# A two-block transformer kernel on one Trainium2 core: the first projections opened feature chunk by feature chunk

## What is computed

```python
mod = jax.nn.silu(c) @ w_ada + b_ada                       # c: 1 x 1024, w_ada: 1024 x 3072
shift, scale, gate = jnp.split(mod[:, None, :], 3, axis=-1)
h = rms_norm(x, norm_g) * (1 + scale) + shift              # 256 x 1024
z = h @ w_in                                               # w_in: 1024 x 2976
c_q, c_kv, k_rope, g_mla, q_b, k_b, v_b, g_moba = jnp.split(z, list(IN_OFFSETS), axis=-1)
o_mla = mla_attention(c_q, c_kv, k_rope, ...)              # needs the 416 latent columns c_q, c_kv, k_rope
o_moba = moba_attention(q_b, k_b, v_b, ...)                # 8 heads of 64: q, k and v have 512 columns each
y = jnp.concatenate([silu(g_mla) * o_mla, silu(g_moba) * o_moba], axis=-1) @ w_out
return x + gate * y
```

## Time and profile before

| | |
|---|---|
| runs | 1599.12, 1601.88 and 2229.82 us; median 1601.88 us |
| profiled execution | 1596.89 us, its span 1594.7 us |
| TensorE busy | 1552.5 us, 97% of the span |
| VectorE, ScalarE busy | 1069.9 and 869.8 us |
| bytes read | 290.57 MB, 183 GB/s over the span |

### The profile page before, as it was taken

How to read it: one execution, slowest core, us unless ns; L and a number is a source line. 1 busy time by engine, 2 the same in 40 slices (tenths; PEclk the granted TensorE clock), 3 DMA queues, 4 the chain that set the end, 5 groups by cost and what they waited for, 6 DMA issues and landing times.

```text
span 1594.7 us, 21371 instructions
## 1 busy us (share of the span) xinstructions
PE 1552.5 (97%) x7540; PEld 1290.8 (81%) x7540; DVE 1069.9 (67%) x1789; ACT 869.8 (55%) x1534; POOL 117.0 (7%) x142
## 2 busy tenths in 40 slices
PE   4989999999999999999999999999999999999998
PEld 4777887788888888888888888888888888888886
DVE  7987877666555766787756557565666578766553
ACT  3676667455445656565644446444566666554442
POOL 0310021011000000021000001000000002100000
PEclk9999999999999999999999999999999999999999
DMA  9964673379854634546565557975463444665651
GB/s 340 322 233 158 196 239 128 104 180 221 222 185 158 198 96 133 174 141 213 197 200 170 198 184 197 199 205 192 158 199 118 139 160 147 211 207 172 205 184 71
DMA packets 149026, 293.03 MB, mean 184 GB/s; under 512 B 10096, under 2 KB 23184, under 8 KB 148920
## 3 DMA queue, kind: packets, MB, share of 16 engines
q1 hardware_dynamic: 143424, 276.60, 51.5%
q0 software_dynamic: 4352, 12.15, 6.2%
q10 hardware_dynamic: 1144, 2.92, 0.5%
HBM read 290.57 MB, written 1.06 MB: 183 GB/s over the span
## 4 chain that ended last, share of the span: by engine, by line
PE 88%; DVE 5%; ACT 3%; issue 2%; DMA 1%; POOL 0%; DVEq 0%; SPq 0%; ACTq 0%
PE pb L475 83%; PE pb L479 5%; DMA raw<-in_w_ada 1%; DVE wl L1529 1%; ACT wh L906 1%; ACT pb L906 1%; DVE mkv L1526 1%; POOL st L2461 0%; DMA raw<-in_w_in 0%; DVE qt L1526 0%; ACT xt_h L906 0%; DVE mk L1529 0%; ACT mkv L906 0%; DVE B L1529 0%; DVE pb L1532 0%
## 5 line engine op out<-in xcount | busy, mean ns | idle before, releaser
L906 ACT ACTIVATE wh<-raw 128x1024 fp32r<-128x1024 f32 (+1 forms) x484 | 506.5, 1053 | 424.6 <-PE pb L475 394.2
L1529 DVE TENSOR_TENSOR wl<-raw,wh 128x1024 fp32r<-128x1024 f32 (+1 forms) x484 | 581.4, 1218 | 197.6 <-ACT wh L906 193.6
L475 PE MATMUL pb<-wh,xt_h 128*128 128x512 f32 (+2 forms) x1472 | 578.1, 393 | 4.0 <-ACT xt_h L906 2.5
L475 PE MATMUL pb<-wh,xt_l 128*128 128x512 f32 (+2 forms) x1472 | 572.4, 389 | 1.4 <-DVE xt_l L1529 1.0
L475 PE MATMUL pb<-wl,xt_h 128*128 128x512 f32 (+2 forms) x1472 | 569.6, 387 | 0.0
L475 PEld LDWEIGHTS pb<-wh,xt_l 128*128 128x128 f32 x1472 | 277.1, 188 | 64.1 <-DVE xt_l L1526 5.9
L475 PEld LDWEIGHTS pb<-wh,xt_h 128*128 128x128 f32 x1472 | 277.2, 188 | 59.5 <-issue 4.0
L475 PEld LDWEIGHTS pb<-wl,xt_h 128*128 128x128 f32 x1472 | 277.4, 188 | 52.5
L475 PE MATMUL pb<-wh,big_h 128*128 128x512 f32 x352 | 137.7, 391 | 0.0
L475 PE MATMUL pb<-wh,big_l 128*128 128x512 f32 x352 | 137.0, 389 | 0.0
L475 PE MATMUL pb<-wl,big_h 128*128 128x512 f32 x352 | 137.0, 389 | 0.0
(11 more groups left out here) (242 smaller groups left out, 1546.5 us busy)
## 6 DMA issues: line engine op xcount, KB each, us to landing
raw<-in_ffn_w_gu SPq DMA_DIRECT2D x160, 512.0 KB, 4.9
raw<-in_w_in SPq DMA_DIRECT2D x148, 512.0 KB, 4.3
raw<-in_ffn_w_down SPq DMA_DIRECT2D x88, 512.0 KB, 3.9
raw<-in_w_ada SPq DMA_DIRECT2D x48, 512.0 KB, 5.3
raw<-in_w_out SPq DMA_DIRECT2D x32, 512.0 KB, 4.1
raw<-in_w_branch SPq DMA_DIRECT2D x24, 512.0 KB, 4.2
raw<-in_ffn_w_gu SPq DMA_DIRECT2D x32, 256.0 KB, 4.9
raw<-in_w_in SPq DMA_DIRECT2D x8, 416.0 KB, 4.8
```

The source lines that it names most:

```text
L475: return e.matmul(o, a, b, start=start, stop=stop)
L906: return e.activation(o, a, func, **kw)
L1529: return e.tensor_tensor(o, a, b, op)
```

## The change

The opening goes by chunks of 128 features. `w_ada` is loaded as column blocks: for feature chunk kx the 1024x128 block of shift and that of scale, each as one transfer of 128 partitions by 8 pieces of 128 columns (512 bytes a piece in HBM). TensorE makes the shift of the chunk from its block: eight products with 128x128 weights and one moving column (`modulation`). DVE sums the scale block in two partial sums (two TENSOR_SCALAR and six SCALAR_TENSOR_TENSOR of 128x128), and TensorE adds these over the partitions with two products against the column of ones (`modulation_sums`). x is loaded first, by SP, and its normalised transpose is kept in SBUF (`x_turned`, over `mkv`). As each chunk is modulated, z, q and k are added up for it, in six banks. The weights of q and k come as one chunk of 1024 columns, those of z as chunks of two feature rows. The v product follows as before. `keep_busy` is gone. The 24 further rows of `w_ada` all come behind v (`later.over(16)`), and the normalisation and turning of the latents, and `mbias`, come after the turning of the q and k heads. ACT issues all its small loads before its first activation.

```diff
+    x_turned = mkv[:, :, :].rearrange("p a b -> p (a b)").rearrange("p (c n) -> p c n", n=256)
+    part_sums = [[acc[:, 512 * i + 128 * z:512 * i + 128 * z + 128] for z in range(2)] for i in range(2)]
+    ACC_Z, ACC_Q, ACC_K = (0, 1), (2, 3), (6, 7)
...
+        def modulation(kx):
+
+            c = shift_at[kx]
+            b = open_bank(4 + kx % 2, ("modk", kx, 1))
+            w.wait_ge(*at(f"raw{c % NRAW}", c))
+            w.wait_ge(*at("csil"))
+            for cc in range(8):
+                last = mm(b[:, 0:1], chunk_view(raw[c % NRAW], c)[:, cc, :], stat(8, "c_silu")[:, cc:cc + 1], cc == 0, cc == 7)
+            last.then_inc(*up("shm", kx))
+            return b
+
+        def modulation_sums(kx, b):
+
+            w.wait_ge(*at("ones"))
+            w.wait_ge(*at("scs", kx, 7))
+            for z in range(2):
+                last = mm(b[:, 1:2], part_sums[kx % 2][z], ones[:, 0:1], z == 0, z == 1)
+            last.then_inc(*up("modm", kx))
...
-        def keep_busy(n):
-
-            w.wait_ge(*at("x"))
-            for _ in range(n):
-                mm(banks[0][:, 0:256], ident, h[:, 0, 0:256], True, True)
...
-        b = rot("cols")
-        w.wait_ge(*at("rows"))
-        tr(b[:, 0:n_rows], rows[0:n_rows, :]).then_inc(*up("rtr"))
-        turn_row(0, 0)
-        turn_row(0, 1)
-        keep_busy(5)
-        list(rows_of_ada(0, 2))
...
+            def blocks(kx):
+                shift_at[kx] = c_no[0]
+                for j, what in enumerate(("shift", "scale")):
+                    if len(plan) == c_no[0]:
+                        plan.append((wa[:, :, DM * j + 128 * kx:DM * j + 128 * kx + 128], 8, 128, None, None, (what, kx)))
+                    c_no[0] += 1
+
+            def weights(kx):
+                if kx % 2 == 0:
+                    zs[0] = take(wi[:, kx:kx + 2, 0:416], 2, 416, ("mm", ("z", 0), 1) if kx == 6 else None)
+                return take(wi[:, kx:kx + 1, 928:1952], 1, DM, ("mm", ("kb", 0), 1) if kx == 7 else None)
...
+            for kx in range(8):
+                qk = weights(kx)
+                if kx < 7:
+                    blocks(kx + 1)
+                for t in range(2):
...
+                    w.wait_ge(*at("xh", ("x", 0), kx))
+                    for nm, i, c, o, hi, lo in parts:
+                        if kx == 0:
+                            open_bank(i, ("eva", (nm, 0), t))
+                        w.wait_ge(*at("hi", c))
+                        mm(o, xh, hi, kx == 0, False)
+                    for nm, i, c, o, hi, lo in parts:
+                        w.wait_ge(*at("lo", c))
+                        mm(o, xh, lo, False, False)
+                    w.wait_ge(*at("xl", ("x", 0), kx))
+                    for nm, i, c, o, hi, lo in parts:
+                        last = mm(o, xl, hi, False, kx == 7)
+                        if kx == 7:
+                            last.then_inc(*up("mm", (nm, 0), t))
+                        elif t == 1 and nm == "z" and kx % 2 or t == 1 and nm == "kb":
+                            last.then_inc(*up("w", c))
+                    if t == 0 and kx < 7:
+                        modulation_sums(kx + 1, modulation(kx + 1))
...
+            gemm(("vb", l), XT, 0, xkey, win, 1952, 512, "eva")
-                later.over(17)
+                later.add(ada(side_tiles[l]), 10 * len(side_tiles[l]))
+                later.over(16)
...
+            for kx in range(8):
+                w.wait_ge(*at("modk", kx, 1))
+                if kx == 0:
+                    w.wait_ge(*at("xev", 1))
+                if kx == 4:
+                    for t in range(2):
+                        w.wait_ge(*at("xevd", t))
+                affine = {"scale": ac[0][:, kx:kx + 1], "bias": mod[:, 0, kx:kx + 1]}
+                ac_(xt_h[:, kx, :], x_turned[:, kx, :], ACT.Identity, **affine).then_inc(*up("xh", ("x", 0), kx))
+                if kx >= 2:
+                    w.wait_ge(*at("xl", ("x", 0), kx - 2))
+                ac_(xtmp[kx % 2], x_turned[:, kx, :], ACT.Identity, **affine).then_inc(*up("xma", ("x", 0), kx))
+                split(stream.lead(3 if kx % 2 else 4))
...
+            if what[0] == "scale":
+                kx = what[1]
+                if kx >= 2:
+                    w.wait_ge(*at("modm", kx - 2))
+                for cc in range(8):
+                    a, b = part_sums[kx % 2][cc % 2], chunk_view(v, c)[:, cc, :]
+                    weight = stat(8, "c_silu")[:, cc:cc + 1]
+                    if cc < 2:
+                        ts(a, b, weight, None, ALU.mult, None).then_inc(*up("scs", kx, cc))
+                        continue
+                    w.wait_ge(*at("scs", kx, cc - 2))
+                    stt(a, b, weight, a, ALU.mult, ALU.add).then_inc(*up("scs", kx, cc))
+                return
...
+            modulation(0)
+            for kx in range(8):
+                if kx:
+                    modulation(kx)
+                split(stream.lead(1 if kx % 2 else 2))
+                w.wait_ge(*at("xh", ("x", 0), kx))
+                w.wait_ge(*at("xma", ("x", 0), kx))
+                tt(xt_l[:, kx, :], xtmp[kx % 2], xt_h[:, kx, :].bitcast(F), ALU.subtract).then_inc(*up("xl", ("x", 0), kx))
+                if kx < 7:
+                    split(stream.lead(2))
...
+            def opening_steps():
+                for t in range(2):
+                    head_scale("qb", 0, (t,))
+                    head_scale("kb", 512, (t,))
+                    yield
+                steps = z_steps()
+                for _ in range(2):
+                    next(steps)
...
+                side.add(opening_steps(), 4)
+                side.over(4)
             gemm(("vb", l), XT, 8, 512, nothing)
             side.drain()
             if l == 0:
-                later.over(17)
+                later.add(ada(side_tiles[l]), 10 * len(side_tiles[l]))
+                later.over(16)
             turn_heads(4)
             turn_heads(4)
+            if l == 0:
+                c_banks = [rot() for c in range(0, 3, 2)]
+                w.wait_ge(*at("gv"))
+                tt(mbias[:, :, :], gv[:, :, ::-1], same_heads(caus, 8), ALU.add).then_inc(*up("mbias"))
+                lower_latents()
...
+        for t in range(2):
+            e.dma_start(h[:, t, :], d["x"][0, t * 128:t * 128 + 128, :]).then_inc(*landed(f"x{t}"))
```

452 lines of the change are left out of this document (220 added, 232 removed).

## The result

The changed kernel takes 1628.57 us (median of four runs, 1627.66 to 1629.36), the kernel before beside it 1600.5 us. That median takes in one slow run of 2229.82 us; the other three are 1598.92, 1599.12 and 1601.88 us, and the ratio, which leaves the slow one out, is 1.018, 95% interval 1.016 to 1.020: 28 to 29 us slower. In the profiled executions the span grew from 1594.7 to 1627.5 us, by 32.8 us. The prediction said 1618 with 1602 to 1634: the direction and the range held, and the middle was 10 us too low. Of the mechanism the first half held, the longer chunk. The second half, that DVE's backlog behind the opening sets the mark, held for a small part of the delay only, as the experiments show.

A forecast was written before the change was run, and what follows sets the result against it. The opening was taken as bound by bytes, TensorE as the bound behind the mark. Opening to 78.5 us, 65 of DVE work and 3 of waits put the mark at 146.5 against 125.3: 1596.9 + 21 = 1618 us, range 1602 to 1634.

The forecast's parts named there:

- the first half: Opening: engines wait for each other in every feature chunk; 51.0 us from the first modulation to the eighth.
- The second half: Behind the opening: DVE's remaining work, not TensorE's 53 us, sets the mark (`mk` scaled), 21 us later than before.
- Product and piece: Opening chunk: a one-column product costs 0.23 us on TensorE; eight 128x128 scale pieces cost 2.0 us on DVE.
- ACT's pieces: Opening chunk: ACT makes `xt_h` and `dg` in 0.41 us each, with a handover of 0.1.
- Start: Start of the opening: first `ac` at 19.9 us, first weight product between 20 and 23 us.
- Clock: Opening: the first chunk and part of the second run at the lower clock level, 4.2 us more.
- Rival 3: Opening: the clock stays at the lower level throughout; 32 us more, 1650 us; chance 0.08.
- v: Behind z, q and k, complete at 81.2 us: v takes 10.9 us of products and is complete at 92.
- The backlog: From the last `xt_l` at 78.5 us: 65 us of DVE work and 3 us of waits put the mark at 146.5.
- Behind the mark: After `mk` is scaled: both kernels are alike and TensorE is the bound, so nothing gives the delay back.

The follow-up runs named there:

- fillers: Changed kernel with five 256-column products whose result nobody reads put into TensorE's first waits; 1629.85 us.
- thin rows: Changed kernel with the side rows of `w_ada` weighed in one column only, the rows still being read; 1624.54 us.
- one shift product: Changed kernel with only one of the eight one-column products of each chunk's shift sum; 1621.96 us.
- long pieces: Changed kernel with the column blocks of `w_ada` in the opening read in pieces of 4 KB instead of 512 bytes; 1629.3 us.

## Why the prediction came out as it did

**Product and piece.** Both prices held. A one-column product costs two records and 0.23 us: 16 records took 1.84 us in every block, as read from the earlier trace rows. The scale block, bounded between two rows of a different shape, took 25.31 to 27.36, 2.05 us against 2.0.

**ACT's pieces.** `xt_h` and `dg` were put at 0.41 each, from a row that copies. They multiply and add, and took:

```profile
L973 ACT ACTIVATE xt_h<-mkv,mod,ac 128x256 fp32r<-128x256 f32 x8 | 4.8, 601 | 39.0 <-DVE ac L1593 39.0
L973 ACT ACTIVATE dg<-mkv,mod,ac 128x256 f32<-128x256 f32 x8 | 4.7, 585 | 0.0
```

That is 0.2 us more each, 0.4 a chunk: an odd chunk is 7.2 us and not 6.8. The trace of before had the nearer row, which I did not use (`z<-pb,mod,ac`, the same size with scale and bias):

```profile
L906 ACT ACTIVATE z<-pb,mod,ac 128x256 f32<-128x256 f32 x4 | 2.2, 558 | 2.0 <-DVE ac L1526 1.9
```

**Start.** First weight product at 23.00, first `ac` complete at 20.9 (predicted 19.9).

**Clock.** 4.2 us were put in for the first chunk and a half. The opening from the first to the eighth modulation took 55.7 us against 51.0 + 4.2, but the terms are not those of the sum: 53.7 at the higher level (2.7 more, ACT's pieces) and 2.0 for the clock, 1.0 of it in the first chunk. Two errors cancel. In the four executions in which the first shift block ran at the lower level it took 57.9, and the clock cost the predicted 4.2. The place held in part only: the lower level comes and goes through the whole opening, at a mean of 0.86 from 30 to 80 us where the kernel before had 1.00, with TensorE busy for the same 47.70 us (47.71 before):

```profile
30.00:80.00 50.00, 47.70 (x241) 39.94 (x239) 27.06 (x77) 17.94 (x26) 0.54 (x2) 0.86 0.93 273
```

```profile
30.00:80.00 50.00, 47.71 (x223) 38.95 (x222) 47.09 (x91) 32.97 (x60) 13.13 (x12) 1.00 0.90 318
```

These two rows (the first of the changed kernel, the second of the one before) are the opening's loss in one view: equal TensorE time, slower and partly spent on single columns, and DVE at 27 instead of 47 us. Rival 3, a clock at the lower level throughout, falls: it was to cost 32 us. The Trainium skill says (TensorE: Matmul & The Clock Gate, Part 1) that the throttled clock is the default, which activity releases. The trace agrees where the fillers stood, for the 16 transposes behind them took 2.74 us and not 3.68; the first chunk was no faster. Why the clock falls in this opening and not in the old one is not settled.

**v.** Predicted complete at 92, measured 102.2. Two things failed in that step. v began at 84.05, not 81.2. And it was counted as 10.9 us without a gap, but the bank of its second half was held by an evacuation that stood on ACT behind a square, which waited for DVE, which was at the angles: 4.27 us, and the lower clock behind it. The prediction foresaw TensorE's wait between v and q0 and not the one inside v. It put 10 us there; from v's end to q0 it is 6.6, of which TensorE waits 3.4 and turns heads and latents for the rest. The wait inside v did no harm to the sum: cutting it by half did not bring q0 forward, since ACT's wait for the weights of `kv` lies behind it.

**The backlog.** This step was mis-sized, and its picture was too simple. 65 us of DVE work and 3 us of waits were to follow the last `xt_l`; it was 66.75 us and 10.05. With an `xt_l` 1.8 late, that makes 1.8 + 1.75 + 7.05 = 10.6, and 146.5 + 10.6 = 157.1. The waits were to be few because of the backlog. But they are not waits for lack of work: DVE runs in order, and ACT is in front of it. The longest, 2.96 us before `wl` at 96.74, has this on ACT's timeline:

```profile
92.36 1.28 ACT L973 ACT_TABLE_LOAD   x1
93.65 0.59 ACT L973 ACTIVATE rope<-ang 128x32 f32<-128x32 f32 x4
94.26 1.28 ACT L973 ACT_TABLE_LOAD   x1
95.55 0.20 ACT L973 ACTIVATE st<-cst 128x1 f32<-128x1 f32 x1
95.66 2.08 ACT L973 ACTIVATE wh<-raw 128x1024 fp32r<-128x1024 f32 x3
```

Two table loads for the sines, 2.56 us, with the upper parts for v behind them. The others are 3.5 us for attention's banks, which q0's slower clock made late (1.62 of it in the row at 115.87), and 1.33 for a square of ACT. My upper bound for the waits was 7.

DVE's work and its waits always add up to the stretch, whatever sets it, so a sum that comes out near is no proof that DVE does. The prediction had q0 behind five rows of `w_ada`; thin rows left q0 where it was, 28.6 us behind the last `xt_l`. Taking 14.4 us of work from DVE shortened the stretch by 4.5 to 6.2 us, moving eight rows away by 1.5. A stretch that DVE's work sets would have shortened by all of it. That 65 us of work fell so close to the length of the stretch is partly luck: with less work for DVE something else, nearly as long, holds the stretch, and what that is from end to end is not shown.

**Behind the mark.** 1470.4 us against 1469.4. In all the kernels of this study this distance lies between 1469 and 1471, so every microsecond at the mark is one at the end.

## What to carry to other kernels

A sum that is turned into a step-by-step feed moves its cost from bytes to a round trip: here ACT, DVE, TensorE and the scale pieces in a ring of 7 to 8 us a chunk, with two such chains within 1 us of each other, so that curing one shows little. Before starting work earlier, ask which engine had the most idle time there and whether the new order still feeds it: here TensorE began 10.8 us sooner, but DVE had done 29 us less by 80 us (37.60 against 23.08 + 43.68), part of it because v was not yet begun. Do not take such a backlog for the loss, though: take its work out and see how far the mark moves. Here it moved by 4 to 6 us of 31.8, while with one shift product the opening ended 5.8 us sooner and the kernel 6.6. And where idle time is to be filled with more transfers, look at which instruction frees the buffer: a ring with a reader that comes late is full long before the memory is.

## What the runs showed of the hardware

- A float32 product with a 128x128 weight and one moving column is two records and as dear as an fp32r product of 512 columns: 0.23 us (1.84 us for 16 records), and 0.43 at the lower clock (3.41 us for 16).
- The clock column of the profile says 1.00 for 20 to 30 us in the kernel with long pieces, while its shift block at 27.23 took 3.41 us, the lower level. Durations are the surer sign.
- Packets of 512 bytes, 16384 more of them than in the long form, cost nothing here at a mean of 273 GB/s from 30 to 80 us (1628.57 us with them, 1629.3 without).
- A copy on ACT of 128x256 takes 0.41 us, the same with scale and bias per partition 0.59 to 0.60 from SBUF and 0.56 from PSUM.
